# Rotary swaps on the sync engine's queue, the last rotation on VectorE, and a reordered opening in a 2-layer hybrid decoder step

## The reference

```
for i in range(2):
    h = rms_norm(x, norm_mix[i])
    z = h @ w_in[i]                        # layer 0: q (12 heads), k, v (4), cross q (4); layer 1: short conv
    layer 0: q, k = rope(rms_norm(q)), rope(rms_norm(k)); o_self = window attention (128) with sinks
    layer 1: o_self = b * conv3(c * u)
    o_x = cross_attend(rms_norm(qx), mem_k[i], mem_v[i])     # 256 memory tokens
    x = x + concat(o_self, o_x) @ w_out[i]
    x = x + square(relu(rms_norm(x) @ w_up[i])) @ w_down[i]
```

## Time and profile before

| | us |
|---|---|
| median of three runs (lowest to highest) | 1163.68 (1163.21 to 1164.44) |
| profiled execution, its own time | 1165.16 |
| its span, first to last instruction | 1163.4 |
| TensorE busy with matmuls in the span | 1143.0 |
| VectorE, ScalarE, GpSimd busy | 781.8, 533.0, 130.4 |
| mean granted TensorE clock, share of full | 0.996 |

### The profile page before, as it was taken

How to read it: one execution, slowest core, us unless ns; L and a number is a source line. 1 busy time by engine, 2 the same in 40 slices (tenths; PEclk the granted TensorE clock), 3 DMA queues, 4 the chain that set the end, 5 groups by cost and what they waited for, 6 DMA issues and landing times.

```text
span 1163.4 us, 22291 instructions
## 1 busy us (share of the span) xinstructions
PE 1143.0 (98%) x9026; PEld 1103.2 (95%) x9026; DVE 781.8 (67%) x1215; ACT 533.0 (46%) x920; POOL 130.4 (11%) x143
## 2 busy tenths in 40 slices
PE   7999999999999999999999999999999999999998
PEld 7899646999999999999999999999999999999998
DVE  5857776798568468568657545689866856756853
ACT  6743886367137227326434222436713722732630
POOL 0018853000000000000240131200000000000000
PEclk8999999999999999999999999999999999999999
DMA  8553231213313222312522321221321331231241
GB/s 309 203 162 119 61 139 61 92 59 124 107 39 112 106 72 102 115 51 94 214 75 73 146 82 66 73 100 56 135 99 48 110 109 72 91 125 43 102 137 48
DMA packets 23866, 120.18 MB, mean 103 GB/s; under 512 B 2788, under 2 KB 7012, under 8 KB 10740
## 3 DMA queue, kind: packets, MB, share of 16 engines
q1 hardware_dynamic: 18612, 100.93, 24.8%
q0 software_dynamic: 1632, 10.54, 2.4%
q10 hardware_dynamic: 3552, 7.74, 2.0%
HBM read 111.29 MB, written 5.69 MB: 101 GB/s over the span
## 4 chain that ended last, share of the span: by engine, by line
PE 88%; DVE 3%; POOL 3%; ACT 2%; issue 2%; DMA 1%; ACTq 1%; SPq 0%; DVEq 0%; POOLq 0%
PE zps L507 48%; PE zps L801 25%; PE ops L801 4%; PE zps L789 4%; POOL sm L1955 2%; PE ops L699 1%; PE tps L671 1%; ACTq L1750 1%; PE zps L545 1%; PE zps L625 1%; ACT w_hi L1445 1%; DMA memx<-memT 1%; DMA tmp<-z 1%; ACT act_hi L1445 0%; DVE sm L1090 0%
## 5 line engine op out<-in xcount | busy, mean ns | idle before, releaser
L507 PE MATMUL zps<-act_hi,w_hi 128*128 128x272 f32 x1664 | 349.2, 291 | 0.0
L507 PE MATMUL zps<-act_hi,w_lo 128*128 128x272 f32 x1664 | 344.3, 288 | 0.0
L507 PE MATMUL zps<-act_lo,w_hi 128*128 128x272 f32 x1664 | 343.5, 288 | 0.0
L801 PE MATMUL zps<-xf,wf 128*128 128x272 f32 x2304 | 297.0, 288 | 0.0
L801 PEld LDWEIGHTS zps<-xf,wf 128*128 128x128 f32 x2304 | 292.2, 188 | 0.8
L507 PEld LDWEIGHTS zps<-act_hi,w_hi 128*128 128x128 f32 x1664 | 262.6, 189 | 4.4 <-issue 2.9
L507 PEld LDWEIGHTS zps<-act_lo,w_hi 128*128 128x128 f32 x1664 | 261.9, 189 | 0.0
L507 PEld LDWEIGHTS zps<-act_hi,w_lo 128*128 128x128 f32 x1664 | 260.1, 189 | 0.0
L1445 ACT ACTIVATE w_hi<-w_stage 128x2048 fp32r<-128x2048 f32 (+2 forms) x65 | 115.6, 1779 | 161.6 <-PE zps L507 122.8
L952 DVE TENSOR_TENSOR w_lo<-w_stage,w_hi 128x2048 fp32r<-128x2048 f32 x57 | 133.4, 2341 | 50.9 <-ACT w_hi L1445 50.6
L1445 ACT ACTIVATE wf<-w_sum 128x1024 fp32r<-128x1024 f32 x64 | 68.0, 1062 | 195.4 <-DVE w_sum L970 90.7
(11 more groups left out here) (193 smaller groups left out, 1279.9 us busy)
## 6 DMA issues: line engine op xcount, KB each, us to landing
w_stage<-wst SPq DMA_DIRECT2D x91, 1024.0 KB, 4.9
kx<-xkT POOLq DMA_DIRECT2D x4, 1024.0 KB, 8.5
vx<-xv POOLq DMA_DIRECT2D x4, 1024.0 KB, 7.4
x_res<-xT ACTq DMA_DIRECT2D x2, 1088.0 KB, 8.3
tmp<-z ACTq DMA_DIRECT2D x32, 68.0 KB, 2.1
yT<-x_res ACTq DMA_DIRECT2D x7, 272.0 KB, 2.0
memx<-memT SPq DMA_DIRECT2D x4, 256.0 KB, 5.2
w_stage<-wst SPq DMA_DIRECT2D x4, 256.0 KB, 5.4
```

What stands on the lines that cost most here:

```text
L507: mm = pe.matmul(zps[slot][:, h, 0:n], w_[:, d, k, w:w + 128], r_[:, k, c0 + h * n:c0 + (h + 1) * n], start=(j == 0 and i == 0), stop=(j = ...
L801: mm = pe.matmul(bank, wf_hl[pw][:, fw, a, :], x_form(l, px, fx, a)[:, 0, :], start=(begin and a == 0 and j == 0), stop=(a == KC // 2 - 1 ...
```

## The change

1. The second weight block, (0, 1), comes in two transfers, with its own semaphore `w3` for the first half.
2. `swapped(r)` moves from ScalarE's queue to SP's, where the swaps stand between weight blocks (4, 0) to (5, 1), behind the write-out of the memory keys.
3. GpSimd rotates seven panels. The eighth (r = 7) is rotated by VectorE (`rotate_last`) before it copies panel 11 out. Scores wait for `r_out` 7 and `r_last`. GpSimd clears `qs` and `qpad0` after its rotations.
4. `colsum(2, NT)` is put into panel 1, behind its second of eight k steps. `turn_keys(2)`, `turn_keys(3)` and their `keys_out` move from panels 1 and 2 to panels 2 and 3.
5. In the opening `norm_hi` and `norm_lo` of k = 0 to 3 come sooner, `add_x0` is spread around the later ones, and `split_hi(2, 1)`, `split_lo(2, 1)` go ahead of `root_keys(2)`, `root_keys(3)` and of `key_sums`, `key_norm` of keys 2 and 3.
6. In VectorE's attention step 7, `product_lo` of step 3 comes after the first of the three `max_pair`s and not after the second.

```diff
@@ sync
-            sp.dma_start(stage[:, 1], wst[1]).then_inc(w_in[1], 16)
+            for h in range(2):
+                c = slice(4 * h, 4 * h + 4)
+                sp.dma_start(stage[:, 1, c], wst[1, :, c]).then_inc(w_in[1] if h else ld["w3"], 16)
+            def swapped(r):
+                sp.wait_ge(n_out, r + 1)
+                if r >= 2:
+                    sp.wait_ge(r_out, r - 1)
+                for to in range(0, 128, 32):
+                    sp.dma_start(tmp[to:to + 32, 4 + r % 2, :], z0[to ^ 32:(to ^ 32) + 32, r, :]).then_inc(r_sw[r % 2], 16)
...
-            weights(Q_ATT + 2, Q_OUT0 + 1)
+            swapped(0)
+            weight(Q_ATT + 2, 0)
+            swapped(1)
+            swapped(2)
+            weight(Q_ATT + 2, 1)
+            swapped(3)
+            swapped(4)
+            weight(Q_OUT0, 0)
+            swapped(5)
+            swapped(6)
+            swapped(7)
+            weight(Q_OUT0, 1)
@@ tensor
-                    pe.wait_ge(r_out, 5 if j == 0 else 8)
+                    pe.wait_ge(r_out, 5 if j == 0 else 7)
+                    if j:
+                        pe.wait_ge(r_last, 1)
...
-                panel(Q_ATT + i // 4, i % 4, *act_hl[0], ready=normed(0) if i == 0 else None)
-                if i == 0:
-                    colsum(2, NT)
-                if i in (1, 2):
-                    turn_keys(1 + i)
+                panel(Q_ATT + i // 4, i % 4, *act_hl[0], ready=normed(0) if i == 0 else None,
+                      between=(lambda k, mm: colsum(2, NT) if k == 1 else None) if i == 1 else None)
+                if i in (2, 3):
+                    turn_keys(i)
@@ vector
+            def rotate_last():
+                z, other = z0[:, 7, :], tmp[:, 5, :]
+                dve.wait_ge(r_sw[1], 64 * 4)
+                dve.tensor_tensor(z, z, cs[:, 0, :], ALU.mult)
+                link(dve.tensor_tensor(other, other, cs[:, 1, :], ALU.mult))
+                dve.tensor_tensor(z, z, other, ALU.add).then_inc(r_last, 1)
...
-                        if p == (0 if j - 4 >= J_LAST - 1 else 1) and 0 <= j - 4 < G_L1:
+                        if p == (0 if j - 4 >= J_LAST - 1 or j - 4 == J_SS + 1 else 1) and 0 <= j - 4 < G_L1:
...
             split_lo_halves(1, 0)
+            norm_lo(0, 0, 0)
             for m in range(2):
                 key_sums(m)
             split_lo(1, 1)
+            for k in range(1, 4):
+                norm_lo(0, k, 0)
             for m in range(2):
                 key_norm(m)
-            for k in range(4):
-                norm_lo(0, k, 0)
             split_lo(2, 0)
+            for k in (1, 2):
+                add_x0(k)
             for k in range(4, KC):
                 norm_lo(0, k, 0)
+            for k in range(3, KC):
+                add_x0(k)
+            split_lo(2, 1)
             for m in (2, 3):
                 key_sums(m)
-            for k in range(1, KC):
-                add_x0(k)
             for m in (2, 3):
                 key_norm(m)
-            split_lo(2, 1)
...
+                if i == 11:
+                    rotate_last()
                 take_scaled(q, p, z0[:, i, :])
@@ scalar
             square_key(0, 1)
+            act.wait_ge(ld["x"], 16)
+            norm_hi(0, 0, 0)
             split_hi(1, 1)
+            for k in range(1, 4):
+                norm_hi(0, k, 0)
             root_keys(0)
             root_keys(1)
             take_memory(0, 2)
             take_memory(0, 3)
-            act.wait_ge(ld["x"], 16)
-            for k in range(4):
-                norm_hi(0, k, 0)
             take_memory(1, 0)
...
+            for k in range(3):
+                square_x0(k)
             act.wait_ge(ld["x1"], 16)
...
             take_memory(1, 3)
-            for k in range(2, KC):
+            for k in range(3, KC):
                 square_x0(k)
+            split_hi(2, 1)
             keys_out(0)
             keys_out(1)
             root_keys(2)
             root_keys(3)
-            split_hi(2, 1)
...
-                if 2 <= i <= 9:
-                    swapped(i - 2)
@@ gpsimd
-            for r in range(8):
-                if r == 7:
-                    pool.wait_ge(n_ms, N_QX[0] + 2)
-                    pool.memset(qs[:, :, :, :], 0.0)
-                    link(pool.memset(qpad0[:, :, :, :], 0.0))
+            for r in range(7):
...
```

More of the change, by code:

```diff
@@ L166, in build_kernel @@
         z_free = [sem(f"z_free{s}") for s in range(2)]
-        ld = {n: sem("ld_" + n) for n in ("con", "con2", "mem0", "mem1", "mem2", "mem3", "w0", "w1", "w2", "x", "x1", "rope", "kt", "vb", "kx0", "kx1", "vx0", "vx1")}
+        ld = {n: sem("ld_" + n) for n in ("con", "con2", "mem0", "mem1", "mem2", "mem3", "w0", "w1", "w2", "w3", "x", "x1", "rope", "kt", "vb", "kx0", "kx1", "vx0", "vx1")}
         m_hi, m_sq, m_los = sem("m_hi"), sem("m_sq"), [sem(f"m_lo{l}") for l in range(2)]
@@ L174, in build_kernel @@
         n_sq, n_ms, n_inv, n_inv2, n_dev, n_out = (sem("n_" + s) for s in ("sq", "ms", "inv", "inv2", "dev", "out"))
-        r_sw, r_out = [sem(f"r_sw{i}") for i in range(2)], sem("r_out")
+        r_sw, r_out, r_last = [sem(f"r_sw{i}") for i in range(2)], sem("r_out"), sem("r_last")
         v_t, v_out = sem("v_t"), sem("v_out")
@@ L455, in _, with weight @@
                 sp.dma_start(stage[:, 0, c], wst[0, :, c]).then_inc(ld[f"w{i}"] if i < 3 else w_in[0], 16)
-            sp.dma_start(stage[:, 1], wst[1]).then_inc(w_in[1], 16)
+            for h in range(2):
[7 more added lines that the diff above has]
+                    sp.dma_start(tmp[to:to + 32, 4 + r % 2, :], z0[to ^ 32:(to ^ 32) + 32, r, :]).then_inc(r_sw[r % 2], 16)
+            def weight(q, d):
+                sp.wait_ge(w_los[d], q)
+                sp.dma_start(stage[:, d], wst[2 * q + d]).then_inc(w_in[d], 16)
             def weights(q0, q1):
@@ L1743, in _ @@
             act.dma_start(con[:, 0:C_IDENT], cst[:, 0:C_IDENT]).then_inc(ld["con"], 16)
[L1744 to L1750, removed]
             def take_memory(l, p):
@@ L1800, in _ @@
                     act.activation(msq[:, k, :], memx[:, k, :], ACT.Square).then_inc(m_sq, 1)
+            act.wait_ge(ld["w3"], 16)
+            copy(w_hi[:, 1, 0:4], stage[:, 1, 0:4]).then_inc(w_his_half, 1)
             act.wait_ge(w_in[1], 16)
-            copy(w_hi[:, 1, 0:4], stage[:, 1, 0:4]).then_inc(w_his_half, 1)
             copy(w_hi[:, 1, 4:8], stage[:, 1, 4:8]).then_inc(w_his[1], 1)
@@ L1831, in _ @@
             take_memory(1, 2)
+            for k in range(3):
+                square_x0(k)
             act.wait_ge(ld["x1"], 16)
[L1833 to L1837, removed]
+            for k in range(4, KC):
                 norm_hi(0, k, 0)
             take_memory(1, 3)
-            for k in range(2, KC):
+            for k in range(3, KC):
                 square_x0(k)
+            split_hi(2, 1)
             keys_out(0)
@@ L1849, in _ @@
                     split_next(Q_ATT + i // 4, i % 4)
-                if i in (1, 2):
-                    keys_out(1 + i)
+                if i in (2, 3):
+                    keys_out(i)
                 if i == 0:
@@ L1988, in _ @@
                 pool.tensor_tensor(z, z, other, ALU.add).then_inc(r_out, 1)
-            pool.wait_ge(r_out, 8)
+            pool.wait_ge(n_ms, N_QX[0] + 2)
+            pool.memset(qs[:, :, :, :], 0.0)
+            link(pool.memset(qpad0[:, :, :, :], 0.0))
             pool.wait_ge(ld["kt"], 16)
+            pool.wait_ge(r_out, 7)
             for hp in range(2):
@@ L1994, in _ @@
             for c in range(6):
+                if c == 5:
+                    pool.wait_ge(r_last, 1)
                 for hf in range(2):
```

## The result

| | before | after |
|---|---|---|
| median, six runs each on one chip (us) | 1164.06 (1162.67 to 1166.35) | 1170.55 (1167.89 to 1170.77) |
| ratio, 95% interval | | 1.0047 [1.0035, 1.0059] |
| profiled execution, its span (us) | 1165.16, 1163.4 | 1167.89, 1166.1 |

The kernel became slower by 5.5 us (the ratio, 0.47%, interval 4.1 to 6.9 us; the two medians lie 6.5 us apart). I had said 1165.4, a difference of +1.7, and a range up to 1167.6: the time lies outside it. The profiled execution of after is the shortest of its six.

What follows compares the result with a forecast made beforehand. TensorE, with matmuls under way for 98% of the span, was taken as the bound. Opening +3.2, swaps -0.7 and low parts -0.8 summed to +1.7 us on the median 1163.68, forecasting 1165.4, range 1162.0 to 1167.6.

Steps and rivals of the forecast that it cites:

- swaps on SP: Moving swaps from ScalarE's queue to SP's: later swaps and weight blocks behind them on SP were costed at 0.
- the cover for the rotations: Seven rotations need finishing only by panel 11's end, so swaps starting later on SP were costed at 0.
- the swaps or the rotation come late: Slower rival: no gain from ScalarE's relief gives +2.4 us, a 4.6 us rotation makes it +3.5; chance 0.10.
- The check named at the prediction's end: Sign of being wrong: panels 6 to 9 wait for weight blocks behind swaps.
- Opening: Column sums, weight split and keys reordered around panels 0 to 2: +3.2 us, between +1.1 and +3.9.
- The chain: ScalarE and VectorE work leading to `headsum(0)`: reciprocal 1.0 us later, at 52.5, and `headsum(0)` at 57.6.
- a start no later than 51.5: Sign of being wrong: VectorE's reciprocal in the opening starts by 51.5 us, against 52.5 predicted.
- The clock: Low TensorE clock after the stand moved behind panel 1: charged 1.7 us, bounds nothing and 2.0.
- TensorE's idle time before panel 1 was slack: The 2.43 us stand before the column sums lay inside the chain to `headsum(0)`, which ends when panel 1 does.
- The 0.70 at a `headsum`: TensorE's wait for late VectorE work, taken as wholly removed by moving swaps to SP: -0.7 us, bounds -0.7 and 0.
- Last rotation: Eighth rotation on VectorE before panel 11's copy: 2.3 us of work fits its 2.78 us stand, so 0.
- Low parts: Attention values: `product_lo` ahead of the second `max_pair` shortens the 1.6 us wait, -0.8 us, bounds -1.6 and 0.

Runs made afterwards that it cites:

- e6_values_late: Changed kernel with the value cache's write-out moved on SP's queue from ahead of the swaps to behind the last weight block; 1166.1 us, ratio 1.0013.
- e2_swaps: Kernel before with only the swaps moved to SP and the last rotation moved to VectorE; 1165.6 us, ratio 1.0000.
- e1_opening: Kernel before with only the halved weight block, column sums inside panel 1, keys turned a panel later and the reordered opening; 1170.06 us, ratio 1.0045.
- e5_keys_back: e1_opening with keys 2 and 3 turned and copied out at panels 1 and 2, as in the kernel before; 1167.6 us, ratio 1.0030.
- e9_order_only: Kernel before with only the new opening order on ScalarE and VectorE, column sums and keys left in place; 1166.95 us, ratio 1.0012.
- e3_low: Kernel before with only the low parts of attention step 3 made one maximum sooner; 1163.57 us, ratio 0.9986.
- e8_colsum_only: Kernel before with only the column sums moved behind the second of panel 1's eight k steps; 1166.23 us, ratio 1.0021.
- e10_old_opening: Kernel before with swaps on SP, last rotation on VectorE, step 3's low parts sooner and the value cache written out late; 1163.05 us, ratio 0.9982.
- e4_after_again: The changed kernel run once more, unaltered, for a second profile; 1169.68 us, ratio 1.0042.

## Why the prediction was wrong, point by point

**The step that failed: "a weight block is wanted by TensorE only panels after it is issued. I cost it at 0"** (swaps on SP), and with it the cover for the rotations. I had seen that `mk_out` would wait one panel longer and that the queue is in order, but not added up what stands on it: the keys' write-out 8.4 us later, the value cache's 992 KB next, which holds the issue behind it for 13.43 us, then the swap, and only then block (4, 0). So the block landed 7.9 us later, its split on VectorE stood in front of the `headsum` chain (0.81 us), and the rotations ended at 129.06, so that GpSimd's clearing and copying of `qs`, and VectorE's last rotation, ended only behind panel 11 (129.78). Measured: 3.4 to 4.0 us by time, 2.8 of it in the profiles, where I had 0 (`e6_values_late`). The swaps on SP by themselves cost nothing that shows (`e2_swaps`, 1.0000), the later keys by themselves some 1.7 us (`e1_opening` against `e5_keys_back`): it is the two on one queue that made the loss. I had the rival, *the swaps or the rotation come late*, at 0.10 and +2.4 to +3.5 in all: right mechanism, too small, since it held no lost clock and no late split. The check named at the prediction's end, panels that wait for weight blocks behind swaps, came near: no panel waited, but ScalarE waited for the block and `headsum(6)` for VectorE.

**Opening, +3.2 predicted, +2.3 in the profile up to `headsum(1)` (+2.5 by `e9_order_only` against `e3_low`), +3.5 by the time of `e5_keys_back`.** The chain: right, the reciprocal 1.1 us later, counted from `split_lo(1, 1)`, where I had 1.0; it started at 51.39 and not at 52.5 because all up to that split ran 1.26 us sooner in this execution (27.91, 29.17 in the earlier trace rows). I had named a start no later than 51.5 as a sign of being wrong; counted from the span's start, as I put it, the sign came, but that start differs between executions (50.02 to 51.55 in four profiles of the old order), so it was badly chosen. The stand of 4.42 us before `headsum(0)` was said to be 4.3. The clock: mis-sized, 1.4 us (8.62 from `headsum(0)` to `headsum(1)`, 7.24 before; one `turn_keys` lies there in both) for my 1.7. The keys turned a panel later: 0.2 us, between `headsum(1)` and `headsum(2)` (7.15, 6.93 before), for my 0.5. That "TensorE's idle time before panel 1 was slack" is shown by `e8_colsum_only` and `e10_old_opening`.

**The 0.70 at a `headsum`, -0.7 predicted:** wrong. It became 0.81, and it was not in every execution of the old order. The Trainium skill (DMA: Bandwidth & Descriptors, "Issuing engines are not separate DMA queues"), which I had set against it, speaks of no more than issue time; `e2_swaps` at 1.0000 fits it, within an interval of 1.0 us to either side.

**Last rotation, 0 predicted:** true where the swaps are on time (`e2_swaps`, `e6_values_late`); in the changed kernel VectorE stood 1.51 us for the swap and began to copy panel 11 at 131.41, 1.6 us behind the panel's end at 129.78 (0.27 before). The rotation itself took 2.2 us, for the 2.3 that I had costed.

**Second weight block, 0 predicted:** nothing is seen; the waits at the memory panels are 7.1 us, 7.2 before.

**Low parts, -0.8 predicted:** the stand went from 1.64 to 0.84 (`e3_low`), as said; the time went by -1.6. No profile with this edit has the low clock at the values, three without it have (`e2`, `e8`, `e9`), at about 1 us for the eight matmuls alone; this may be the other half.

**Open:** the profile accounts for 3.8 us of the 5.5, and five of its six executions took 2.2 us or more longer than the profiled one. Their mean granted clock was 0.992 to 0.994, against its 0.995, so stretches of low clock that the profile does not have are the likely place; where they lie was not seen, and `e4_after_again`, a second profile, has the same stands and no further one. What `e8_colsum_only` lost by time is open too.

## What to carry to other kernels

When a write-out on an in-order queue comes to wait for a later event, follow the queue to the next load behind it and add up every byte ahead of that load; here one 992 KB write-out that nobody waited for stood before a weight block, and did little harm there until what stood ahead of both came 8.4 us later. A stand that is only slack inside a longer chain moves when its work is moved; shorten the chain (here the reciprocal ahead of a split that is wanted later) and the time follows. Take a gain from a small stand only if more than one execution shows it.

## What the runs showed that I had not expected

The granted clock does not follow from a stand's length alone: after 2.43 us before the column sums it fell to 0.50, after 2.45 us at the same place in `e10_old_opening` it stayed 1.00; after 1.64 us at the values it stayed full before, after 1.65 us in `e2_swaps` it fell. Nor was a longer stand always followed by it: after 2.70 us before `headsum(0)` in `e9_order_only` the clock fell to 0.50, after 3.26 us at the same place in `e8_colsum_only` it stayed 1.00. And a transfer's issue can be what is slow. Whatever SP issued next behind the value cache was held: a weight block 10.50 us (before) and 10.70 (`e1_opening`), four swaps of 68 KB 13.43 (after) and 13.51 (`e2_swaps`), and a write-out (`o_kp`) 10.96 where the value cache was moved ahead of it (`e6_values_late`); without it ahead the block took 0.6 us, the four swaps 3.67 and `o_kp` 0.67. During the 13.43 us the DMA engines were busy for only two to three tenths of most of the time.
